# Modulation blocks of a four-layer transformer kernel at other places in TensorE's order

## The chip, the cores and the metric

The kernel runs on one core of a Trainium2 chip. The metric is the time of one execution on the device in microseconds (us); "before" is the median of three runs. The engines are TensorE (PE, matrix products), VectorE (DVE), ScalarE (ACT), GpSimd (POOL) and SyncE (SP, which here only issues transfers). Each has a queue of its own and works it off in order; a wait on a semaphore holds up everything behind it in that queue.

## What is computed

Two layers of a first block on 256 latent and 256 context tokens of width 1024, then two layers of a second block on the latent tokens alone. The change touches the first block:

```python
for i in range(DEPTH):                      # 2 layers
    mod_l = jnp.split((jax.nn.silu(c) @ w_mod[i] + b_mod[i])[:, None, :], N_MOD, axis=-1)      # 6 parts
    mod_c = jnp.split((jax.nn.silu(c_ctx) @ w_mod[i] + b_mod[i])[None, None, :], N_MOD, axis=-1)
    h_l = modulate(rms_norm(x, norm1_g[i]), mod_l[0], mod_l[1])
    h_c = modulate(rms_norm(ctx, norm1_g[i]), mod_c[0], mod_c[1])
    ...  # i == 0: diff_attention_mixer; i == 1: neighbourhood_mixer
    x = x + mod_l[2] * y_l
    x = x + mod_l[5] * squared_relu_mlp(modulate(rms_norm(x, norm2_g[i]), mod_l[3], mod_l[4]), w_mlp1[i], w_mlp2[i])
    ...  # the same for ctx with mod_c, in layer 0
```

`w_mod[i]` has 1024 x 6144 elements. The vectors `c` and `c_ctx` are the same for all tokens, so a product with it is two rows against a large matrix: the work lies in bringing its weights in: 24 blocks of 1024 x 256 elements a layer.

## The kernel before

All numbers are fp32. A product with full accuracy is made of three passes (`passes`, L802 where it issues the matmuls) over a weight block split into a high and a low part: ACT rounds a block of the ring to `Wh` (L1523), DVE writes the rest to `Wl` (L2044), each in two halves; the same is done to activations (`HTh`, `HTl`).

**The ring.** All weights of the program form one list, `blocks`, built by `first_weights` and `second_weights` in the order in which SP issues their transfers (L2806). The ring has RING = 3 slots of 1 MB; block i goes to slot i % 3, so its transfer waits until block i - 3 has left: when it is a split block, until DVE has split its second half (semaphore `w_split`), when it is a raw one, until PE has used it (`mod_used`). There are two buffers of split weights (SPLIT = 2).

**Modulation.** A modulation block is 256 columns of `w_mod`, a raw block of 1 MB. `modulation_block` (L956) multiplies it without a split, eight matmuls of 32 x 256 into the accumulator bank `mod_sum` (pa3), with `cT` on the other side. The first eight blocks of layer 0 are taken at the start, in another form. The 40 later ones (`LATER_MOD`) are called by `next_modulation(n)` from PE's program: n = 0 to 19 (`QK_MOD` = 20), one behind each tile of the first layer's query, key and value projections; n = 20 to 39 in steps of the first attention (`modulation_step`: steps 0, 1, 3, 5 and 6 of each eight). Blocks form groups (`MOD_GROUPS`); when one is complete, ACT copies its sums (`copy_group`), PE folds them (`fold_group`), ACT copies the result and DVE adds the bias (`add_group`) into `MOD`. DVE's `gains` makes the norms' factors from `MOD`. While groups are open, bank pa3 is theirs, and the pool A of accumulators has three banks in place of four (`A.width`); after the first attention it has four again.

**Norms.** In a norm PE sums the squares (`norm`, the matmuls with `con` and `Pb` or `Lb`), ACT makes the root, and DVE and ACT write eight normed tiles (`normed`, L2136, L1567, L2143). PE's first product behind a norm takes a tile as soon as it is there (`side_by_side`). Around a norm the order on DVE is: the first half of the second weight block (`prepare((0,))`, by `last=(0,)`), the root, the eight tiles, then the second half of that block (`prepare((1,))`).

**Near attention** (layer 1) has 16 steps of two heads each (`NEAR_STEPS`). Step s on PE is the scores of s, the transposes of s - 2 and the values of s - 3. Its bias tables come by `bias_rows(c)`, 16 transfers of 64 KB in pieces of 64 elements: c = 0 and 1 from POOL's queue, c = 2 and 3 from SP's, at the place in `blocks` that `late_bias` names, when the last value tile is complete.

## Time and profile before

| | us |
|---|---|
| median of three runs | 2641.91 (2641.17 to 2642.12) |
| profiled execution, its own time | 2639.67 |
| its span, first to last instruction | 2637.9 |
| PE busy | 2508.2 (95%) |
| DVE busy | 1701.9 (65%) |
| ACT busy | 1234.5 (47%) |
| POOL busy | 234.4 (9%) |
| TensorE's mean granted clock | 0.981 of 2.4 GHz |

In the trace the first layer's projections run from about 45 to 234 us, the first attention to 337, the second norm of layer 0 stands at 377, the first norm of layer 1 at 737, and the near attention runs from 879 to 937. A timeline row reads: start, duration, engine, line, operation, written <- read, and in brackets how long the engine was idle before it and what ended that. Matmuls overlap, so the time that one takes from PE is the distance between two starts, not its duration.

### The profile page before, as it was taken

How to read it: one execution, taken by the hardware profiler on the slowest of the kernel's cores; microseconds unless marked ns; L12 is line 12 of the kernel's file. 1: busy time of each engine (PE TensorE's matmuls, PEld its weight loads, DVE VectorE, ACT ScalarE, POOL GpSimd, SP SyncE). 2: the span in 40 equal slices, each digit the busy share in tenths (PEclk: the TensorE clock that was granted, in tenths of full speed). 3: DMA queues.
4: the chain of work that ended last, by engine and by line, in shares of the span. 5: the costliest groups of instructions: out<-in, count | busy, mean ns of one | idle time of the engine just before them, and what ended most of it. 6: DMA issues, size and time to landing. Idle time of an engine off the chain costs nothing.

```text
span 2637.9 us, 41664 instructions
## 1 busy us (share of the span) xinstructions
PE 2508.2 (95%) x16871; PEld 2221.6 (84%) x16871; DVE 1701.9 (65%) x3153; ACT 1234.5 (47%) x2228; POOL 234.4 (9%) x277
## 2 busy tenths in 40 slices
PE   6999989999989999999999999999999999999998
PEld 4666578888877689999989979899899899798997
DVE  4664855545575666677657677776676576777764
ACT  3433733223255554454444455554544444555443
POOL 1000010000053310000010012000000100120001
PEclk8999999999989999999999999999999999999999
DMA  7655723223235335556564525465765644254654
GB/s 269 208 172 193 225 77 112 96 96 96 96 89 119 80 111 164 164 173 176 166 173 148 153 74 176 128 192 162 206 177 168 172 147 154 77 175 128 189 166 122
DMA packets 497135, 393.74 MB, mean 149 GB/s; under 512 B 26168, under 2 KB 464704, under 8 KB 496048
## 3 DMA queue, kind: packets, MB, share of 16 engines
q1 hardware_dynamic: 494144, 384.92, 48.1%
q0 software_dynamic: 2080, 3.53, 1.1%
q8 instruction: 134, 2.20, 0.4%
q10 hardware_dynamic: 720, 2.62, 0.3%
q14 instruction: 57, 0.47, 0.1%
HBM read 389.99 MB, written 1.05 MB: 148 GB/s over the span
## 4 chain that ended last, share of the span: by engine, by line
PE 84%; DVE 9%; ACT 3%; issue 1%; SPq 1%; DMA 1%; POOL 1%; DVEq 0%; ACTq 0%
PE pv L802 35%; PE pa L802 31%; PE pv L1266 6%; PE pv L767 4%; PE pv L1265 3%; DVE Wl L2044 3%; PE pa L767 2%; PE pa L772 2%; ACT Wh L1523 1%; PE pa L956 1%; SPq L2790 1%; DMA BIG<-in_w_mod_dram 0%; DVE HTl L2051 0%; POOL BIG L2764 0%; DVE TMP L2136 0%
## 5 line engine op out<-in xcount | busy, mean ns | idle before, releaser
L2044 DVE TENSOR_TENSOR Wl<-ring,Wh 128x1024 fp32r<-128x1024 f32 (+4 forms) x688 | 757.8, 1142 | 269.6 <-ACT Wh L1523 266.2
L1523 ACT ACTIVATE Wh<-ring 128x1024 fp32r<-128x1024 f32 (+4 forms) x688 | 641.1, 980 | 497.1 <-PE pv L802 329.9
L802 PE MATMUL pa<-HTl,Wh 128*128 128x256 f32 (+1 forms) x1648 | 540.7, 328 | 34.8 <-DVE HTl L2143 20.9
L802 PE MATMUL pv<-HTl,Wh 128*128 128x256 f32 (+1 forms) x1872 | 539.3, 288 | 16.0 <-DVE T L2478 5.9
L802 PE MATMUL pv<-HTh,Wh 128*128 128x256 f32 (+1 forms) x1872 | 537.6, 287 | 0.0
L802 PE MATMUL pv<-HTh,Wl 128*128 128x256 f32 (+1 forms) x1872 | 537.5, 287 | 0.0
L802 PE MATMUL pa<-HTh,Wl 128*128 128x256 f32 (+1 forms) x1648 | 522.6, 317 | 0.0
L802 PE MATMUL pa<-HTh,Wh 128*128 128x256 f32 (+1 forms) x1648 | 522.0, 317 | 0.0
L802 PEld LDWEIGHTS pa<-HTl,Wh 128*128 128x128 f32 x1648 | 320.9, 195 | 69.0 <-issue 42.4
L802 PEld LDWEIGHTS pv<-HTl,Wh 128*128 128x128 f32 x1872 | 359.8, 192 | 21.8 <-issue 11.8
L802 PEld LDWEIGHTS pv<-HTh,Wh 128*128 128x128 f32 x1872 | 359.9, 192 | 2.5
L802 PEld LDWEIGHTS pv<-HTh,Wl 128*128 128x128 f32 x1872 | 359.9, 192 | 2.4
L802 PEld LDWEIGHTS pa<-HTh,Wl 128*128 128x128 f32 x1648 | 321.1, 195 | 20.3 <-issue 1.4
L802 PEld LDWEIGHTS pa<-HTh,Wh 128*128 128x128 f32 x1648 | 320.6, 195 | 18.5
L1266 PE MATMUL pv<-HID,Wh 128*128 128x512 f32 x704 | 246.9, 398 | 0.0
L2703 POOL TENSOR_TENSOR Pb<-Pb 128x256 f32<-128x256 f32 (+1 forms) x60 | 62.6, 1044 | 1452.9 <-ACT Pb L1534 1452.0
L1265 PE MATMUL pv<-HID,Wl 128*128 128x256 f32 x672 | 189.0, 281 | 0.0
L802 PE MATMUL pv<-HID1h,Wl 128*128 128x512 f32 (+1 forms) x512 | 172.1, 336 | 0.0
L802 PE MATMUL pv<-HID1l,Wh 128*128 128x512 f32 (+1 forms) x512 | 172.1, 336 | 0.0
L802 PE MATMUL pv<-HID1h,Wh 128*128 128x512 f32 (+1 forms) x512 | 172.1, 336 | 0.0
L2173 DVE SCALAR_TENSOR_TENSOR XT<-pv,MOD,XT 128x256 f32<-128x256 f32 x216 | 95.6, 479 | 112.0 <-PE pv L802 111.2
L1266 PEld LDWEIGHTS pv<-HID,Wh 128*128 128x128 f32 x704 | 130.6, 188 | 29.9
(277 smaller groups left out, 3309.5 us busy)
## 6 DMA issues: line engine op xcount, KB each, us to landing
ring<-in_ffn_w_gu_dram SPq DMA_DIRECT2D x176, 512.0 KB, 5.1
ring<-in_w_mlp_dram SPq DMA_DIRECT2D x64, 1024.0 KB, 5.3
ring<-in_ffn_w_down_dram SPq DMA_DIRECT2D x64, 704.0 KB, 4.6
ring<-in_w_in_dram SPq DMA_DIRECT2D x42, 1024.0 KB, 5.2
ring<-in_w_mod_dram SPq DMA_DIRECT2D x40, 1024.0 KB, 5.6
ring<-in_a_w_qkv_dram SPq DMA_DIRECT2D x12, 1024.0 KB, 5.2
ring<-in_b_w_qkv_dram SPq DMA_DIRECT2D x12, 1024.0 KB, 5.2
ring<-in_w_out_dram SPq DMA_DIRECT2D x8, 1024.0 KB, 5.1
```

The lines of the kernel that those rows point to most:

```text
L767: m = nc.tensor.matmul(o, lhsT=lhsT, rhs=rhs, start=start, stop=stop)
L772: m = nc.tensor.transpose(o, x, C("ident"))
L802: m = nc.tensor.matmul(o, lhsT=x, rhs=y, start=first and j == 0, stop=last and j == 2)
L956: m = nc.tensor.matmul(mod_sum[32 * j:32 * j + 32, 0:256], lhsT=cT[:, k, 30 - 2 * at:62 - 2 * at], rhs=w[:, k, :], start=at == 0 and k < 4 ...
L1265: nc.tensor.matmul(b[:, 0:S], lhsT=wl[:, k, :], rhs=HID2h[:, kk, :], start=False, stop=False)
L1266: m = nc.tensor.matmul(b.rearrange("p (a n) -> p a n", a=2), lhsT=wh[:, k, :], rhs=HID2[:, :, kk, :], start=kk == 0, stop=kk == 2 * half - 1)
L1523: ins = nc.scalar.activation(Wh[rows, p % SPLIT, a:b], ring[rows, i % RING, a:b], ACT.Copy)
L2044: ins = v.tensor_tensor(Wl[rows, p % SPLIT, a:b], ring[rows, i % RING, a:b], Wh[rows, p % SPLIT, a:b].bitcast(F32), ALU.subtract)
L2173: m = v.scalar_tensor_tensor(XT[:, k, half], b[:, at:at + S], MOD[:, i, gate * KT + k, w:w + 1], XT[:, k, half], ALU.mult, ALU.add)
L2703: nc.gpsimd.tensor_tensor(a, a, squares(k)[:, 0:N], ALU.add).then_inc(sum_ready, 1)
L2790: sp.dma_start(dst, I["w_mod"][0][k * P:(k + 1) * P, a * width:(a + 1) * width]).then_inc(mod_in[k], 16)
```

## The change

The 40 later modulation blocks are placed anew: 8 with the projections (at the places `QK_PLACES`), 16 in the first attention (every second step, without step 16), 3 behind the sums of the second norm of layer 0, 3 behind those of the first norm of layer 1, 10 in steps 1 to 10 of the near attention. In the list of transfers the three of a norm stand behind the two weight blocks of the product that follows it; those of the near attention stand behind the first two of its output weight's four blocks. The groups of blocks and the steps at which they are copied, folded and added follow. With it:

- Pool A keeps three banks until step 15 of the near attention; one of the four value tiles of layer 1 goes to pool V and is copied by DVE.
- SP issues the bias tables ahead of the near attention's modulation blocks: c = 2 before the first three, c = 3 before the other seven. It waits for the value tile in pool V.
- `cT`, `modtwo`, `modt` and `fold` lie in the place of the last constants, which are loaded in the MLP of layer 1 (`last_consts`, `const_last`); "ones" is half as wide.
- Layer 1's gains of the second norm are made behind the near attention.

```diff
-QK_MOD = 20
+QK_PLACES = (0, 1, 3, 6, 9, 12, 15, 17)
+QK_MOD = len(QK_PLACES)
+HOLE_MOD = 3
...
-    places = (0, 1, 3, 5, 6)
-    n = QK_MOD + i // 8 * 5 + (places.index(i % 8) if i % 8 in places else -99)
-    return n if QK_MOD <= n < LATER_MOD else None
-
-
-MOD_GROUPS = ((0, FIRST_MOD), (FIRST_MOD, 16), (FIRST_MOD + 16, 16), (FIRST_MOD + 32, 8))
...
+    n = i // 2 if i < 16 else 8 + (i - 18) // 2
+    return QK_MOD + n if i % 2 == 0 and i != 16 and n < 16 else None
+
+
+AFTER_DIFF = QK_MOD + 16
+NEAR_MOD = AFTER_DIFF + 2 * HOLE_MOD
+MOD_GROUPS = ((0, FIRST_MOD), (FIRST_MOD, 16), (FIRST_MOD + 16, 8), (FIRST_MOD + 24, 16))
...
+                modulation_columns(QK_MOD, AFTER_DIFF)
+                by_columns(I["a_w_o"][0], 0, D)
             else:
-                by_columns(w, 0, 2 * D)
+                by_columns(w, 0, 512)
+                modulation_columns(NEAR_MOD - HOLE_MOD, NEAR_MOD)
+                by_columns(w, 512, 2 * D)
                 for c in range(2):
                     halves_of_rows(w, 2 * D + c * 512, 512)
-            by_columns(I["a_w_o" if i == 0 else "b_w_o"][0], 0, D)
-            if i == 1:
-                late_bias.append(len(blocks))
+                by_columns(I["b_w_o"][0], 0, 512)
+                late_bias.append(len(blocks) - 1)
+                modulation_columns(NEAR_MOD, NEAR_MOD + 3)
+                late_bias.append(len(blocks) - 1)
+                modulation_columns(NEAR_MOD + 3, LATER_MOD)
+                by_columns(I["b_w_o"][0], 512, D)
+                last_consts.append(len(blocks) + 6)
             n = CHUNK * P
             for c in range(FF1 // n + 1):
                 if c < FF1 // n:
                     by_columns(I["w_mlp1"][i], c * n, (c + 1) * n)
+                if c == 0 and i == 0:
+                    modulation_columns(AFTER_DIFF, AFTER_DIFF + HOLE_MOD)
...
-            return [(V if i == 0 and t == 3 else A, ("v", i, c, t)) for t in range(4)]
+            return [(V if t == 3 else A, ("v", i, c, t)) for t in range(4)]
...
+                    if 1 <= s <= LATER_MOD - NEAR_MOD:
+                        next_modulation(NEAR_MOD + s - 1)
...
+                    if s == NEAR_FOLDED:
+                        fold_group(3)
+                        A.width = BANKS
...
                     norm(("n1", i), ALL)
+                    for n in range(NEAR_MOD - HOLE_MOD, NEAR_MOD):
+                        next_modulation(n)
...
                 if i == 0:
-                    pe.wait_ge(mod_copied, len(MOD_GROUPS))
-                    A.width = BANKS
+                    A.width = BANKS - 1
                 norm(("n2", i), tc)
+                if i == 0:
+                    for n in range(AFTER_DIFF, AFTER_DIFF + HOLE_MOD):
+                        next_modulation(n)
...
-                    sp.wait_ge(a_full, A.nth(("v", 1, 1, 3)))
-                    for c in (2, 3):
-                        for dst, src in bias_rows(c):
-                            sp.dma_start(dst, src).then_inc(bias_late[c - 2], 16)
+                    c = late_bias.index(i)
+                    sp.wait_ge(v_full, V.nth(("v", 1, 1, 3)))
+                    for dst, src in bias_rows(2 + c):
+                        sp.dma_start(dst, src).then_inc(bias_late[c], 16)
+                if i in last_consts:
+                    sp.wait_ge(mod_added, len(MOD_GROUPS))
+                    sp.dma_start(con[:, LAST_CONST:CONST_W], I["pack"][:, LAST_CONST:CONST_W]).then_inc(const_last, 16)
```

SP's queue from the first attention's last modulation blocks to the MLP of layer 0, before; a row is a transfer into the ring, with its shape, what it waits for, and how many follow each other (`w_mod` modulation, `a_w_o` the output weight, `w_mlp` the MLP's two weights):

```order
L2806 DMA ring<-in_w_mod_dram 128x8x256 [waits mod_used] x19
L2806 DMA ring<-in_a_w_o_dram 128x8x256 [waits mod_used] x3
L2806 DMA ring<-in_a_w_o_dram 128x8x256 [waits w_split]
L2806 DMA ring<-in_w_mlp_dram 128x8x256 [waits w_split] x4
L2806 DMA ring<-in_w_mlp_dram 128x4x512 [waits w_split] x2
```

The same, in the changed kernel:

```order
L2849 DMA ring<-in_w_mod_dram 128x8x256 [waits mod_used] x13
L2849 DMA ring<-in_a_w_o_dram 128x8x256 [waits mod_used] x3
L2849 DMA ring<-in_a_w_o_dram 128x8x256 [waits w_split]
L2849 DMA ring<-in_w_mlp_dram 128x8x256 [waits w_split] x2
L2849 DMA ring<-in_w_mod_dram 128x8x256 [waits w_split] x3
L2849 DMA ring<-in_w_mlp_dram 128x8x256 [waits mod_used] x2
L2849 DMA ring<-in_w_mlp_dram 128x4x512 [waits mod_used]
```

Three modulation blocks now stand behind the MLP's first two, each waiting for a split block to leave its slot; on PE they stand between the norm's sums (`pa<-Lb,con`) and the first product, and in layer 1 it is the same:

```order
L793 MATMUL pa<-Pb,con 128x512
L793 MATMUL pa<-Lb,con 128x512
L982 MATMUL pa<-ring,con 32x256 x24
L828 MATMUL pa<-HTl,Wh 128x512
L828 MATMUL pa<-HTh,Wl 128x512
```

That is PE in the changed kernel at the second norm of layer 0; the row of 24 is new there.

SP's queue around the near attention, before (`b_w_o` is its output weight, `b_rpb` the bias tables):

```order
L2806 DMA ring<-in_b_w_o_dram 128x8x256 [waits w_split] x4
L2806 DMA ring<-in_w_mlp_dram 128x8x256 [waits w_split]
L2813 DMA HTf<-in_b_rpb_dram 64x4x64 [waits a_full]
L2813 DMA HTf<-in_b_rpb_dram 64x4x64 x15
L2813 DMA Oa<-in_b_rpb_dram 64x4x64 x16
L2806 DMA ring<-in_w_mlp_dram 128x8x256 [waits w_split] x3
```

And in the changed kernel:

```order
L2849 DMA ring<-in_b_w_o_dram 128x8x256 [waits w_split] x2
L2856 DMA HTf<-in_b_rpb_dram 64x4x64 [waits v_full]
L2856 DMA HTf<-in_b_rpb_dram 64x4x64 x15
L2849 DMA ring<-in_w_mod_dram 128x8x256 [waits w_split] x3
L2856 DMA Oa<-in_b_rpb_dram 64x4x64 [waits v_full]
L2856 DMA Oa<-in_b_rpb_dram 64x4x64 x15
L2849 DMA ring<-in_w_mod_dram 128x8x256 [waits mod_used] x7
L2849 DMA ring<-in_b_w_o_dram 128x8x256 [waits mod_used] x2
```

The modulation blocks stand behind the bias transfers there, and half of the output weight behind them.

## Rows read from the trace of the kernel before

**Rows 1.** The page: the span, and TensorE's (PE's) busy time

```profile
span 2637.9 us, 41664 instructions
...
PE 2508.2 (95%) x16871; PEld 2221.6 (84%) x16871; DVE 1701.9 (65%) x3153; ACT 1234.5 (47%) x2228; POOL 234.4 (9%) x277
```

**Rows 2.** PE timeline, first projections, and values' end: start us, us, work [idle before]

```profile
96.76 1.07 PE L956 MATMUL pa<-ring,BIG 128*32 128x256 f32 x16
...
97.76 0.50 PE L802 MATMUL pa<-HTl,Wh 128*128 128x512 f32 x1
...
104.20 0.59 PE L767 MATMUL pv<-BIG,con 128*128 128x256 f32 x2
...
233.64 1.07 PE L956 MATMUL pa<-ring,BIG 128*32 128x256 f32 x16
```

**Rows 3.** Timelines of ACT and DVE, the first projections

```profile
96.55 2.00 ACT L1523 ACTIVATE Wh<-ring 128x1024 fp32r<-128x1024 f32 x2
...
102.51 0.75 DVE L2345 SCALAR_TENSOR_TENSOR BIG<-BIG,gq,RQ 128x512 f32<-128x512 f32 x1
```

**Rows 4.** Timelines of PE, SyncE's queue (SPq) and ACT, first attention

```profile
296.07 0.63 PE L772 MATMUL pa<-con,Pb 128*128 128x128 f32 x4 [0.77 <-DVE HTl L2215]
...
312.92 0.37 SPq L2806 DMA_DIRECT2D ring<-in_a_w_o_dram  x1
...
320.52 1.05 ACT L1523 ACTIVATE Wh<-ring 128x1024 fp32r<-128x1024 f32 x1
...
324.74 1.16 PE L767 MATMUL pa<-BIG,PT 128*128 128x128 f32 x8 [1.25 <-ACT PT L1600]
```

**Rows 5.** Timelines of PE, DVE and SPq, second norm of layer 0

```profile
383.65 0.77 PE L802 MATMUL pa<-HTl,Wh 128*128 128x512 f32 x1 [6.48 <-DVE HTl L2143]
...
388.91 0.51 PE L802 MATMUL pa<-HTl,Wh 128*128 128x512 f32 x1
...
394.93 1.22 DVE L2044 TENSOR_TENSOR Wl<-ring,Wh 128x1024 fp32r<-128x1024 f32 x1
...
396.18 0.37 SPq L2806 DMA_DIRECT2D ring<-in_w_mlp_dram  x1
...
397.20 0.39 PE L802 MATMUL pa<-HTl,Wh 128*128 128x512 f32 x1
```

**Rows 6.** Timelines of PE, DVE and SPq, first norm of layer 1

```profile
743.30 0.55 PE L802 MATMUL pa<-HTl,Wh 128*128 128x256 f32 x1 [5.90 <-DVE HTl L2143]
...
750.45 1.22 DVE L2044 TENSOR_TENSOR Wl<-ring,Wh 128x1024 fp32r<-128x1024 f32 x1
...
751.70 0.37 SPq L2806 DMA_DIRECT2D ring<-in_b_w_qkv_dram  x1
...
751.84 0.70 PE L767 MATMUL pa<-SQ,con 128*128 128x256 f32 x2 [0.39 <-ACT SQ L1721]
```

**Rows 7.** Timelines of ACT, SPq and PE, near attention

```profile
877.90 0.60 ACT L1600 ACTIVATE BIG<-pa 128x512 f32<-128x512 f32 x1 [2.12 <-PE pa L802]
...
882.28 10.60 SPq L2813 DMA_DIRECT2D HTf<-in_b_rpb_dram  x16
...
882.76 2.55 PE L767 MATMUL pv<-BIG 64*128 64x512 f32 x4 [2.02 <-DVE nm L2284]
...
892.92 11.34 SPq L2813 DMA_DIRECT2D Oa<-in_b_rpb_dram  x16
...
895.51 1.13 PE L767 MATMUL pv<-BIG 64*128 64x512 f32 x4
...
898.62 1.13 PE L767 MATMUL pv<-BIG 64*128 64x512 f32 x4
...
909.59 1.21 PE L772 MATMUL pa<-con,Pb 128*128 128x128 f32 x8 [0.35 <-DVE Pb L2291]
```

**Rows 8.** DMA issues: KB each, median us to landing; and a window's DMA share, GB/s

```profile
ring<-in_w_mod_dram SPq DMA_DIRECT2D x40, 1024.0 KB, 5.6
...
892.00:896.00 4.00, 4.00 (x40) 2.54 (x38) 3.23 (x13) 2.92 (x7) 1.30 (x2) 1.00 0.64 96
```

More of the change, by code:

```diff
@@ L126, in constant_pack @@
     put("eps", np.full((P, 1), EPS))
-    put("minus", -np.ones((P, P)))
+    t = np.arange(S)
+    qc, kc = p % GRID_W, t % GRID_W
+    start = np.clip(qc - NA_COLS // 2, 0, GRID_W - NA_COLS)
+    inside = (kc[None, :] >= start[:, None]) & (kc[None, :] < start[:, None] + NA_COLS)
+    back = p // GRID_W * GRID_W + GRID_W - 1 - qc
+    put("ncol", np.where(inside, 0.0, NEG)[back])
+    half = HEAD // 2
+    freq = np.power(np.float32(10000.0), -np.arange(half, dtype=np.float32) * np.float32(2.0 / HEAD)).astype(np.float32)
+    put("freq", freq[p % half][:, None])
     pb = np.zeros((P, P))
```

77 lines of the change are left out of this document (42 added, 35 removed).

## The prediction

> **What bounds the kernel now.** I read the page first, then TensorE's own timeline stage by stage, then the waits. TensorE (PE) is busy for 95% of the span [rows 1], so a stage is worth looking at only where PE stops, or where something PE does can leave its queue. A modulation block is 16 overlapping matmul records; in the projections of the first layer one runs from 96.76 to 97.76, so it holds PE for 1.00 us [rows 2]. The 40 later blocks are about 40 us of PE. All 40 stay; what changes is where they stand, and what must have happened before each of them. A block is not split: PE reads it straight from the ring, so it needs a landed transfer of 1 MB, issue to landing 5.6 us in the median [rows 8], and the transfer needs a free one of three ring slots.
>
> **Part 1, projections of the first layer: 20 blocks become 8.** PE runs there without a gap: block, eight steps of a tile, the sum of squares, the turned pairs, block [rows 2]. Twelve removals are worth 12 x 1.00 = 12.0 us, less two things. The last removed block, at 233.64, stands where PE would wait for the last value tile's copy on VectorE anyway [rows 2]; I count 0.2 of its 1.0 us. And behind the odd tiles the turned pairs become the next wait: there ScalarE first splits a weight block (96.55) and VectorE ends the tile's gain at 103.26, while PE comes at 104.20 [rows 2, 3]. That is 0.94 us of slack, and the block taken away is 1.00 us, so four odd tiles lose 0.1 to 0.2 us each, 0.6 in all. Sum: 12.0 - 0.8 - 0.6 = **-10.6 us**, from -12 (neither counts) to -8 (1 us lost at each of the four).
>
> **Part 2, first attention: 20 blocks become 16.** PE is the bound here too: its only waits in the steady part are of 0.77 us, once in eight steps [rows 4]. Before, the blocks of steps 0 and 1 cost nothing (PE would wait for the first softmax); afterwards those of step 0 and step 32 don't, the latter because PE waits 1.25 us near it [rows 4]. So 18 paid blocks become 14: -4.0. Against it: the output weight's first block takes the ring slot of the block of step 28, before that of step 27. It was issued at 312.92 and ScalarE split it at 320.52 [rows 4]; a step of 2.5 to 3.8 us later, plus 5.6 us, it lands at 321 to 322, and ScalarE stands before it for about 1.5 us with the transposed copies behind. Sum **-2.5 us**, from -4.5 to +1.
>
> **Part 3, the hole of the second norm of layer 0: three blocks.** PE stops at 377.17 and starts the next product at 383.65, 6.48 us later, when VectorE has written the first normed tile; three blocks of 1.00 us would fit [rows 5]. But the order of the transfers decides. The ring holds three blocks; in it stand o3, u0, u1 (the last block of the output weight, the first two of the MLP); behind them come the three modulation blocks. The first takes o3's slot, the second u0's, the third u1's. A slot of a split block is free when both halves are split, and VectorE does the second half of u1 only behind all eight normed tiles: 394.93 plus 1.22. The row of SyncE shows it: the block that now takes u1's slot is issued at 396.18 [rows 5]. In the new order that block is the third modulation block, and PE has it ahead of the first MLP product. It lands at 396.18 + 5.3 to 5.6 = 401.6; PE, at the low clock after 22 us of standing (the profile shows 12 matmuls at 0.43 us from 383.65 to 388.91, then 0.227 us), needs 1.6 us for the block and 12.5 us for the 48 matmuls of u0: 415.6. Now the next product follows at 397.20 [rows 5]. VectorE does not wait for PE in the norm, so nothing moves that transfer forward. **+18.5 us**, from +15 to +22 (landing 4.6 to 7 us, 1 to 3 us of clock).
>
> **Part 4, the hole of the first norm of layer 1: three blocks.** The same construction: the third block takes the slot of the second projection block, whose second half VectorE splits at 750.45 to 751.67, behind the normed tiles; SyncE issues at 751.70 [rows 6]. Two gain operations of about 0.2 us leave VectorE ahead of the norm, so 751.3; landed at 756.8; block and 48 matmuls, 5 us of it at the low clock, end at 765.1. Now the two tiles are through at 751.4 (743.30 plus 48 matmuls) [rows 6]. +13.7. In this layer the pool of accumulators also has three banks where it had four, since the modulation sum keeps the fourth: a product then waits for the root of the tile three before it. Behind odd tiles ScalarE needs copy, square, split and root (0.2 + 0.5 + 2.0 + 1.6 us) in a PE step of 3.3 us, some 0.9 us too much, once in the part where PE isn't held by VectorE already. **+14.7 us**, from +12 to +19.
>
> **Part 5, the near attention: ten blocks.** A step is 3.11 us of PE without a gap (895.51, 898.62) [rows 7], so a block in it costs its 1.00 us. Worse is the first. SyncE's queue is in order: the last value product ends at 877.9; now SyncE issues 16 bias transfers in 10.60 us and 16 more in 11.34 us [rows 7], and nobody waits for SyncE behind them. In the new order three modulation blocks stand behind the first 16 and seven behind the second 16, and PE has one in each of steps 1 to 10. So: bias issued 878.0 to 888.7, first block landed at 894.3, where PE has been waiting since 884.5; with the blocks at 897 and 901 (they share the transfer engines with the second bias set) the scores of step 4 start at 904.4 instead of 892.40. The second 16 are issued by 901.2, the fourth block lands at 906.7: 1.2 us more of wait. Seven blocks at 1.00 us: +7.0. Gone are PE's three short waits behind that, the first of them 0.35 us [rows 7], some 1.2 us. 12.0 + 1.2 + 7.0 - 1.2 = **+19.0 us**, from +12 to +26. The value tile that moves to VectorE delays the first scores from 878.76 to 882.4, under the same wait.
>
> The Trainium skill (DMA: Bandwidth & Descriptors, section on issuing engines not being separate DMA queues) says that the sequencer's time to initiate a DMA is usually small relative to the DMA itself. By that rule the first block would be on its way soon after 878 and this part would come to +7. The trace doesn't bear it out for bias pieces: 0.66 us each.
>
> **The rest** I count at nothing: the constants' order (the last ones are loaded in the MLP of layer 1, 300 us ahead of their use; the new 0.4 us issue stands among transfers that PE has two blocks ahead), the gains now behind the near attention (VectorE idles there until the first output product), three banks in the MLP of layer 0 (a product of 5.4 us there against a 0.6 us copy).
>
> **Sum.** -10.6 - 2.5 + 18.5 + 14.7 + 19.0 = **+39.1 us**. The profiled execution took 2639.67 us (span 2637.9 and 1.8 around it); 2678.8. The median of the three timed runs is 2.24 us above the profiled one, so I expect 2641.9 + 39.1 = **2681.0 us**.
>
> **Rivals.**
> A. *The blocks are there in time and the holes get filled* (faster). Speaks for it: the hole is 6.48 us long, two of the three blocks do find their slots free early, and while PE works it keeps its clock (the twelve slow matmuls, 2.4 us, would go in each hole). Against it: SyncE's issue at 396.18 and 751.70. It decides at whether the third block is landed by 383.65. Then part 3 is 0 to -2.4, part 4 +1 to -1.4, and if the blocks of the near attention come in time as well, that part is ten blocks less PE's two waits at its start (2.02 and 0.7 us [rows 7]), +7.3: -10.6 - 2.5 - 1.2 - 0.2 + 7.3 = -7 us, 2635. Chance 0.04.
> B. *The near attention hides its first block's wait* (the blocks go out before the bias, or the issues are quick): +7, total +27, 2669. Against it stands the queue's order. Chance 0.15.
> C. *The transfers get in each other's way*: bias rows are 256-byte pieces and kept the transfer engines 0.64 busy for 96 GB/s [rows 8]; with blocks between them each of the first four may land 3 us later, and the three banks cost a wait at every odd tile. +10 and +5, total +54, 2696. Chance 0.10.
> D. *Only one of the two holes stalls*, since something I read as a wait isn't one there: 2662 to 2666. Chance 0.05.
> The Trainium skill (TensorE: Matmul & The Clock Gate, section on HAM oscillation) advises to keep DMA waits out from between matmuls, since the engine runs at the low clock behind each. What the low clock takes is in the terms from the rows; the page alone would only add that PE comes out slow after every such wait.
>
> **How the numbers follow.** Forecast 0.66 (2671 to 2691), A 0.04, B 0.15, C 0.10, D 0.05. Range for 8 in 10: 2664 to 2695, which takes in B and most of C. A measurement of this kernel tells about 0.2% (5 us) from no change. Faster 0.03 (most of A), same 0.02 (the rest of it, and a near attention that eats its gain), slower 0.95.
>
> **What would show it.** In the new profile: PE idle for about 22 us before the third block of the first hole and 17 us in the second, released by the transfer into the ring, and SyncE's issue of that block right behind VectorE's split of the block two before; PE idle about 10 us after the second scores of the near attention, with 16 bias issues ahead on SyncE; the projections at 6.96 us a tile where no block stands. I am wrong if PE works through either hole, if the third block is issued before VectorE's normed tiles, or if the projections keep 7.96 us a tile.

## The result: 2.4% slower, 63 us where 39 were forecast

| | before | after |
|---|---|---|
| median of the timed runs, us (lowest to highest) | 2642.01 (2641.17 to 2645.80) | 2705.24 (2701.61 to 2707.09) |
| profiled execution, us (span) | 2639.67 (2637.9) | 2706.05 (2704.3) |
| mean granted clock of TensorE in it | 0.981 | 0.969 |

The ratio is 1.0241, with a 95% interval of 1.0229 to 1.0253. The direction and the two holes were right; the time lies 10 us above the range of the forecast. The page of the changed kernel, to be held against [rows 1]: PE has as many matmuls, is busy 8.5 us longer, and its share of the span falls from 95% to 93%. So nearly all of the loss is standing.

```profile
span 2704.3 us, 41666 instructions
...
PE 2516.7 (93%) x16871; PEld 2229.1 (82%) x16871; DVE 1705.5 (63%) x3155; ACT 1233.7 (46%) x2226; POOL 237.9 (9%) x277
...
PEclk8999989999989799999999999999999999999999
```

**Where the time went.** In both kernels ScalarE writes 688 halves of weight blocks (the tile Wh), in the same order. The start of the k-th one in a trace, less its start in the trace of before, is the distance that the kernel has lost up to there. Two such pairs, the first and last lines of the part behind the near attention (timeline of ACT; first before, then after):

```profile
943.87 2.01 ACT L1523 ACTIVATE Wh<-ring 128x1024 fp32r<-128x1024 f32 x2 [6.74 <-PE pv L802]
...
2349.03 2.01 ACT L1523 ACTIVATE Wh<-ring 128x1024 fp32r<-128x1024 f32 x2 [1.99 <-PE pv L802]
```

```profile
1000.50 2.01 ACT L1558 ACTIVATE Wh<-ring 128x1024 fp32r<-128x1024 f32 x2 [6.86 <-PE pv L828]
...
2415.47 2.01 ACT L1558 ACTIVATE Wh<-ring 128x1024 fp32r<-128x1024 f32 x2 [3.30 <-PE pv L828]
```

1000.50 - 943.87 = 56.6 and 2415.47 - 2349.03 = 66.4 us: 9.8 us are lost in stages that the prediction counted at nothing. The same difference at five marks (before's clock: 209, 342, 739, 878, 944, 2349 us) gives this table; every experiment below is read by it. Each column is what the stage added to the distance, in us, in one profiled execution.

| kernel | projections (to 209) | first attention | hole of norm 2, layer 0 | hole of norm 1 and projections, layer 1 | near attention | behind it | sum |
|---|---|---|---|---|---|---|---|
| forecast | -10.6 | -2.5 | +18.5 | +14.7 | +19.0 | 0 | +39.1 |
| after | -9.8 | +0.2 | +18.7 | +12.2 | +35.3 | +9.8 | +66.4 |
| e1_split_ahead | -11.1 | +0.7 | -0.2 | +3.6 | +33.5 | +8.4 | +34.9 |
| e2_bias_behind | -12.0 | -0.4 | +18.0 | +11.5 | +27.0 | +7.6 | +51.7 |
| e3_both | -13.0 | -1.6 | -1.2 | +2.9 | +26.5 | +8.3 | +21.8 |
| e4_delay | -2.3 | 0.0 | +0.1 | +0.1 | 0.0 | +41.0 (the added copies) | +38.8 |
| e5_even | -10.0 | -1.5 | +18.1 | +11.5 | +35.2 | +4.9 | +58.2 |
| e6_bias_pool | -10.1 | -0.4 | +18.0 | +11.5 | +27.4 | +7.3 | +53.6 |
| e7_all | -9.9 | 0.0 | -0.1 | +1.0 | +29.9 | +8.0 | +28.8 |
| e8_att_cut | -10.9 | -1.5 | +18.0 | +14.7 | +35.4 | +9.7 | +65.4 |
| e9_old_columns | -11.2 | 0.0 | +17.7 | +11.4 | +33.1 | +1.1 | +52.1 |
| e10_interleave | -9.3 | -0.4 | -0.9 | +3.0 | +20.3 | +7.8 | +20.4 |
| e11_holes_only | -0.5 | +1.1 | +0.1 | +1.0 | 0.0 | +2.5 | +4.2 |
| e12_small_blocks | -11.0 | 0.0 | +0.5 | +1.5 | +5.5 | +8.3 | +4.9 |
| e13_gap15 | -9.6 | +0.1 | +18.9 | +12.3 | +35.4 | +2.6 | +59.8 |
| e14_paid_places | -4.5 | +2.9 | -0.2 | +1.1 | -0.1 | +0.7 | 0.0 |
| e15_before_column | +0.5 | +0.1 | +0.2 | +0.1 | +0.4 | +10.2 | +11.4 |

The first column shows how far such numbers can be trusted: twelve kernels have the projections of the changed kernel (all but e4, e11, e14 and e15), and they lie between -9.3 and -13.0; e4 has those of the kernel before, and stands at -2.3. A difference under 3 us in one cell is not read as an effect.

Two marks need care. The first, at 209, lies ahead of the last three of the 20 places of the projections. ScalarE's first softmax of the first attention (237.23 before, 226.13 after) is the better border: counted there, the changed kernel has won 11.1 us in the projections and lost 1.5 in the first attention. And the mark at 739 is the write of a second half, which e1, e3, e7, e10 and e12 move ahead of the norm. By PE's last sums of that norm (736.81 before) e1 has +1.8 in the first hole and +1.6 behind it, where the table says -0.2 and +3.6; in the other four the same 2 us pass from the one column to the other.

**The holes**, to be held against [rows 5, 6]. First hole, timelines of PE, DVE and SyncE's queue:

```profile
367.50 1.94 PE L982 MATMUL pa<-ring,con 128*32 128x256 f32 x32
...
391.82 1.93 PE L982 MATMUL pa<-ring,con 128*32 128x256 f32 x16 [22.39 <-DMA ring<-in_w_mod_dram]
```

```profile
385.33 1.22 DVE L2081 TENSOR_TENSOR Wl<-ring,Wh 128x1024 fp32r<-128x1024 f32 x1
...
386.58 0.37 SPq L2849 DMA_DIRECT2D ring<-in_w_mod_dram  x1
```

Two blocks (32 records) run at once, PE stands for 22.39 us, and the third block's transfer is issued 0.03 us after VectorE has split the second half of the block two before it. The second hole is the same picture: 17.98 us, and an issue at 761.03 behind a split that ends at 761.00.

**The near attention**, against [rows 7]. PE's timeline, then SyncE's queue:

```profile
904.06 3.78 PE L793 MATMUL pv<-BIG 64*128 64x512 f32 x8 [4.41 <-DVE BIG L2063]
...
919.18 1.94 PE L982 MATMUL pa<-ring,con 128*32 128x256 f32 x16 [11.34 <-DMA ring<-in_w_mod_dram]
...
926.92 1.07 PE L982 MATMUL pa<-ring,con 128*32 128x256 f32 x16 [0.79 <-DMA ring<-in_w_mod_dram]
...
940.60 1.93 PE L982 MATMUL pa<-ring,con 128*32 128x256 f32 x16 [9.50 <-DMA ring<-in_w_mod_dram]
```

```profile
899.68 10.60 SPq L2856 DMA_DIRECT2D HTf<-in_b_rpb_dram  x16
...
910.32 6.11 SPq L2849 DMA_DIRECT2D ring<-in_w_mod_dram  x3
...
916.48 15.36 SPq L2856 DMA_DIRECT2D Oa<-in_b_rpb_dram  x16
...
931.88 11.08 SPq L2849 DMA_DIRECT2D ring<-in_w_mod_dram  x4
```

The first set of bias transfers takes SyncE 10.60 us, as before. But the three blocks behind it take SyncE 6.11 us (the third issue alone 4.84), the second bias set 15.36 us where it took 11.34, and there is a second long wait of 9.50 us before the fourth block, for which the forecast had 1.2. Blocks after a wait last 1.93 us, not 1.07: PE has fallen to the low clock. Stretches of 4 us there (PE, PEld, DVE, ACT, POOL busy; granted clock; share of the transfer engines; GB/s):

```profile
916.00:920.00 4.00, 0.82 (x8) 0.40 (x12) 0.00 (x0) 0.00 (x0) 0.00 (x0) 0.50 1.10 365
...
940.00:944.00 4.00, 3.40 (x23) 2.13 (x24) 0.00 (x0) 0.38 (x1) 0.00 (x0) 0.50 1.08 342
944.00:948.00 4.00, 4.00 (x32) 2.40 (x34) 0.94 (x4) 0.81 (x2) 0.00 (x0) 0.66 0.90 304
```

In the last microseconds before the first block lands (PE has it at 919.18) the transfer engines are taken up wholly.

### The profile page after: what moved, and what is told of

It reads as the page before. It is cut to its first block, busy times and chain, and to the rows that moved or that the text cites. A ratio compares the mean times of both kernels' runs of the same rounds, so it can differ in the third digit from the quotient of the medians.

```text
span 2704.3 us, 41666 instructions
## 1 busy us (share of the span) xinstructions
PE 2516.7 (93%) x16871; PEld 2229.1 (82%) x16871; DVE 1705.5 (63%) x3155; ACT 1233.7 (46%) x2226; POOL 237.9 (9%) x277
## 4 chain that ended last, share of the span: by engine, by line
PE 81%; DVE 9%; ACT 3%; SPq 2%; issue 2%; DMA 2%; POOL 1%; DVEq 0%; ACTq 0%; POOLq 0%
PE pv L828 34%; PE pa L828 29%; PE pv L1301 6%; PE pv L793 4%; PE pv L1300 3%; DVE Wl L2081 2%; PE pa L793 2%; ACT Wh L1558 2%; PE pa L798 1%; PE pa L982 1%; SPq L2856 1%; SPq L2833 1%; DMA ring<-in_w_mod_dram 1%; DVE TMP L2173 1%; DVE HTl L2180 1%
## 5 line engine op out<-in xcount | busy, mean ns | idle before, releaser
L828 PEld LDWEIGHTS pa<-HTh,Wl 128*128 128x128 f32 x1648 | 321.2, 195 | 20.4 <-issue 1.4
```

The source lines that it names most:

```text
L828: m = nc.tensor.matmul(o, lhsT=x, rhs=y, start=first and j == 0, stop=last and j == 2)
```

## Experiments

All runs were made beside runs of the kernel before on the same chip (medians 2640.75 to 2641.48 us), in four series.

**e1_split_ahead: who holds the third block of a hole**

```
-  residual_gated(o ..., last=(0,)); norm_mod(n2); prepare((1,))
+  residual_gated(o ..., last=(0, 1)); norm_mod(n2)          # the same for n1 of layer 1, and on ScalarE
```

> The changed kernel, but in both holes ScalarE and VectorE split the second half of the MLP's (the projections') second block ahead of the norm, not behind its eight tiles. Theory 1 (the third modulation block waits for that ring slot, as parts 3 and 4 of the prediction say): SyncE issues the third block some 2 us after the norm's squares, it lands 5.5 us later, and PE stands for 0 to 4 us before it in place of 22.4 and 18.0. The two holes give back 15 to 18 and 10 to 14 us, 28 in all, near 2677 us. The norm itself comes about 1.2 us later. Rival (the transfer is slow or queued for another reason, or PE's clock is the cost): the waits before the third block stay above 12 us and the time stays within 8 us of 2705.

Measured: 2674.91 us, ratio 1.0127 [1.0112, 1.0142], 30 us below the changed kernel. PE's timeline at the two holes:

```profile
374.27 1.93 PE L982 MATMUL pa<-ring,con 128*32 128x256 f32 x16 [5.65 <-DMA ring<-in_w_mod_dram]
```

```profile
737.15 1.94 PE L982 MATMUL pa<-ring,con 128*32 128x256 f32 x16 [6.49 <-DMA ring<-in_w_mod_dram]
```

The waits fell from 22.39 and 17.98 to 5.65 and 6.49 us, a little longer than the 4 us of the expectation, and SyncE issued the block at 368.94. The two holes, the second with its projections, now cost 1.8 and 1.6 us in place of 18.7 and 12.2. So the cause of parts 3 and 4 is shown: the slot, freed by a split that stood behind the norm.

**e2_bias_behind and e3_both: the order on SyncE**

```
   by_columns(b_w_o, 0, 512)
-  [16 bias] M0 M1 M2 [16 bias] M3 ... M9
+  M0 M1 M2 [16 bias] M3 M4 M5 [16 bias] M6 ... M9          # M: a modulation block's transfer
```

> The changed kernel, but on SyncE the first three modulation blocks of the near attention stand ahead of the first 16 bias transfers, and the next three ahead of the second 16. Theory 1 (what the near attention pays is the order on SyncE, with 16 issues of 0.66 us or more in front of the blocks): the waits of 11.34 and 9.50 us are gone, that stage comes to 7 to 12 us above the kernel before in place of 34.9, and the time to some 2680 us. Rival (bias pieces and blocks get in each other's way in the transfer engines whatever the order): PE still stands for 5 us or more at a block of this stage, the stage stays above +20 and the time above 2690.

> Both edits at once. If the two causes are independent, the gains add: 28 + 25 us below the changed kernel, near 2652 us, and what is left over the kernel before is the late part (some 10 us) and the blocks that PE pays. If an earlier stage only hands its wait to the next, the gains don't add, and the time stays above 2665.

Measured: 2693.18 us (1.0200 [1.0183, 1.0218]) and 2665.15 us (1.0089 [1.0074, 1.0104]). The gains of the two edits add (30 + 12 against 40), though e3_both stays at the 2665 us that the expectation had named for the opposite: the second edit is worth 12 us and not 25. But the near attention only fell from 35.3 to 27.0 and 26.5, not to 7 to 12. In e3_both PE has the first three blocks at once, then waits 5.36 us for the fourth and 7.48 us for the seventh. The rival of e2_bias_behind had said just that: over 5 us at a block, stage above +20, time above 2690.

**e6_bias_pool: the bias transfers on GpSimd's queue**

```
-  sp.wait_ge(v_full, ...); 32 x sp.dma_start(bias)
+  pool.wait_ge(v_full, ...); 16 x pool.dma_start(bias)       # ahead of its steps; then 4 in each of steps 0 to 3
```

> The changed kernel, but GpSimd's queue issues the last 32 bias transfers, 16 ahead of its first step of the near attention and four in each of its first four steps; SyncE has only blocks. Theory 1 (the order on SyncE is what the near attention pays): PE's waits of 11.34 and 9.50 us before blocks are gone, what is left is 10 us of blocks, the 4.4 us wait for the value tile and 1 to 2 us of low clock, +12 us over the kernel before in that stage in place of +34.9: near 2682 us. Rival (the transfers get in each other's way in the engines): with the bias set in flight at the same moment PE still waits 5 us or more before a block, and the stage stays above +20.

Measured: 2697.26 us (1.0212 [1.0196, 1.0227]), the stage +27.4. No block is waited for any more; PE waits for GpSimd, which scales the second head's softmax. GpSimd's timeline, and the wait on PE:

```profile
897.60 9.18 POOL L2779 DMA_DIRECT2D HTf<-in_b_rpb_dram  x15 [35.06 <-PE pv L828]
914.94 0.62 POOL L2779 DMA_DIRECT2D HTf<-in_b_rpb_dram  x1 [8.15 <-issue]
...
918.02 0.70 POOL L2786 TENSOR_SCALAR Pb<-Pb,rr 128x512 f32<-128x512 f32 x1
```

```profile
918.78 1.12 PE L798 MATMUL pa<-con,Pb 128*128 128x128 f32 x4 [9.05 <-POOL Pb L2786]
```

Fifteen issues run in a row (0.61 us each), then the queue stands for 8.15 us before the sixteenth. I take it that something behind the issues is full; no row says what. Both theories missed: the waits left the blocks, as the first said, and the loss stayed, as the second said.

**e7_all: four edits at once** (the splits ahead, GpSimd's queue, the even column of e5, and on VectorE)

```
-  prepare(); copy_in(value_tiles(1, 1)[3])
+  copy_in(value_tiles(1, 1)[3]); prepare()
```

> Four edits at once: the splits ahead of the norms, the last bias transfers by GpSimd, the even column, and VectorE copies the last value tile ahead of its split of the output weight's block (in the changed kernel PE waits 4.41 us for that copy at the first scores). If all four causes are as I take them, they add: 2665 (both first edits) less 15 to 19 in the near attention less 5 to 7 late, 2638 to 2645 us, level with the kernel before. If it stays above 2650, one of the causes isn't what I take it for.

Measured: 2668.85 us (1.0107 [1.0092, 1.0122]), 24 us more than expected. Two of the four causes weren't what I took them for: the near attention stayed at +29.9 (PE waits 13.85 and 6.09 us for GpSimd's products behind its issues), and the even column did nothing. The copy did its part: the wait before the first scores went from 4.41 to 1.08 us.

**e10_interleave and e12_small_blocks: issue time or transfer time**

```
+  M0 M1 M2 [8 bias] M3 [4 bias] M4 [4 bias] ... M8 [4 bias] M9    # e10, with the edits of e1 and the copy of e7
+  block_of(..., (0, 1, ...))  for M0 to M9                        # e12: one row tile of eight is loaded
```

> The changed kernel with the splits ahead of the norms and the value tile's copy first, and with SyncE's queue of the near attention mixed: three blocks, eight bias transfers, block, four bias transfers, block, and so on. Theory 1 (a bias transfer costs its queue 0.6 to 0.7 us wherever it is issued, and what is paid is only what stands in a row ahead of a block or of GpSimd's own steps): four of them, 2.7 us, fit into a step of 4.1 us, PE's waits before blocks fall below 1 us, and the stage costs 8 to 12 us over the kernel before (26.5 with three blocks in a row ahead of 16 transfers); near 2649 us. Rival (transfer engines): waits of 5 us or more stay before blocks or products, the stage stays above +20, the time above 2660.

> The kernel e10 with one difference: each of the ten blocks' transfers in the near attention loads only the first of its eight row tiles (128 KB of 1 MB); the other seven tiles are left out, and PE multiplies what the slot held. Issues, waits and matmuls are the same in number. Theory 1 (blocks of 1 MB and bias pieces share the transfer engines, which are the bound of that stage: SyncE's first issue behind each block took 2.3 to 3.6 us in place of 0.62): these long issues vanish, PE's waits of 5.01 to 0.8 us before blocks go, the stage costs 10 to 12 us over the kernel before in place of 20.3; near 2650 us. Rival (the issues themselves on one queue are the bound): the waits stay, and the time stays within 3 us of 2660.

Measured: e10_interleave 2659.99 us (1.0070 [1.0058, 1.0083]), stage +20.3, not 8 to 12, with a wait of 5.01 us before a block, as the rival had said. SyncE's queue in it:

```profile
874.63 5.34 SPq L2860 DMA_DIRECT2D HTf<-in_b_rpb_dram  x8
880.01 0.60 SPq L2851 DMA_DIRECT2D ring<-in_w_mod_dram  x1
880.66 4.42 SPq L2860 DMA_DIRECT2D HTf<-in_b_rpb_dram  x4
885.12 0.60 SPq L2851 DMA_DIRECT2D ring<-in_w_mod_dram  x1
885.77 5.52 SPq L2860 DMA_DIRECT2D HTf<-in_b_rpb_dram  x4
```

The first eight bias issues take 0.67 us each. Once blocks are between them, four take 4.42 to 6.04 us, since one issue behind each block takes 1.7 to 3.6 us. The six blocks issued between bias transfers take 9.1 to 10.2 us from issue to landing (5.6 in the median of the kernel before [rows 8]), and PE's step of 4.1 us has become one of 5.0 to 6.4. Then e12_small_blocks, the same issues with an eighth of the blocks' bytes: 2643.57 us (1.0009 [1.0000, 1.0018]), stage +5.5 (less than the 10 to 12 of the expectation), no wait before any block, and 3.6 to 4.7 us from issue to landing. Its queue:

```profile
878.72 0.60 SPq L2854 DMA_DIRECT2D ring<-in_w_mod_dram  x1
879.37 2.59 SPq L2863 DMA_DIRECT2D HTf<-in_b_rpb_dram  x4
882.00 0.60 SPq L2854 DMA_DIRECT2D ring<-in_w_mod_dram  x1
882.64 2.58 SPq L2863 DMA_DIRECT2D HTf<-in_b_rpb_dram  x4
```

This decides it. With the bytes the six groups of four cost 4.4 to 6.0 us (5.2 in the mean), without them 2.6 to 3.1: what is paid is transfer time that blocks and bias pieces share. 32 bias transfers of 0.66 us and ten blocks of about 2.6 us (5.2 less 2.6, an estimate) are 21 + 26 = 47 us of transfers, for a stage of 16 steps whose blocks PE wants within the first eleven. The Trainium skill (DMA: Bandwidth & Descriptors, section on issuing engines not being separate DMA queues) says that transfers of all issuing engines end on the same 16 DMA engines. e6 agrees: with the bias on another queue the waits moved to another engine, and the stage only fell from 35.3 to 27.4 us. The +5.5 of e12 is ten blocks of 1.00 us, less 1.8 us of PE's waits in the stage (5.0 before, 3.1 in e12), less what the kernel before pays there at the low clock and e12 doesn't. That leaves 2.7 us for the clock; from the rows it is 0.49 x 3.33 + 0.36 x 4.00 = 3.1, an estimate:

```profile
884.00:888.00 4.00, 3.33 (x12) 1.69 (x10) 3.82 (x18) 3.17 (x9) 1.13 (x2) 0.51 0.98 288
888.00:892.00 4.00, 4.00 (x24) 2.33 (x26) 2.17 (x11) 2.44 (x7) 0.82 (x2) 0.64 0.70 120
```

```profile
880.00:885.00 5.00, 5.00 (x58) 3.05 (x51) 3.65 (x17) 3.44 (x9) 0.98 (x1) 1.00 0.65 122
```

The first two rows are the kernel before, the last is e12.

**e4_delay, e5_even, e9_old_columns, e13_gap15, e15_before_column: the 9.8 us behind the near attention**

```
e4   before: + for _ in range(100): step(v.tensor_copy(NT, XT[:, 0]))   # behind the near attention
e5   after:  + put("gap", zeros((P, 1)))    ahead of "halves", 1 column at the end
e9   after:  + put("gap", zeros((P, 255)))  ahead of "halves", 1 column at the end
e13  after:  + put("gap", zeros((P, 15)))   ahead of "halves", 1 column at the end
e15  before: "freq" (1 column) put ahead of "halves"
```

> The kernel before with one addition: 100 copies of 128x512 on VectorE, one behind the other, between the near attention and the next residual, about 60 us in which PE stands. No work of the stages behind it is changed. Theory 1 (the late 9.8 us of the changed kernel are PE's clock, which depends on when a short wait falls): the distance to the kernel before grows or falls by 2 to 10 us between that point and the end, in steps right behind waits of 2 to 3 us, at a lower granted clock. Rival (the late 9.8 us come from the change's own edits: constants, banks, gains): the distance stays the same within 1 us up to the end.

Measured: 2679.20 us (1.0144 [1.0129, 1.0160]). PE stood for 38.15 us more; the distance was 38.65 us at 994 and 38.65 to 38.8 at the end. This shift costs nothing later, so the first theory fell: the 9.8 us had to come from the change's own edits. That sent me to the durations, line by line, of the stages behind. One difference stands out. The page's groups of GpSimd's products with the constant "before" (a mask), in the kernel before and in the changed one:

```profile
L2769 POOL TENSOR_TENSOR TMP<-TMP,con 128x512 f32<-128x512 f32 x10 | 11.2, 1121 | 9.0 <-ACT TMP L1912 8.9
L2764 POOL TENSOR_TENSOR BIG<-BIG,con 128x512 f32<-128x512 f32 x10 | 10.9, 1092 | 388.8 <-DVE BIG L2569 388.8
```

```profile
L2812 POOL TENSOR_TENSOR TMP<-TMP,con 128x512 f32<-128x512 f32 x10 | 13.1, 1308 | 8.5 <-ACT TMP L1949 8.5
L2807 POOL TENSOR_TENSOR BIG<-BIG,con 128x512 f32<-128x512 f32 x10 | 12.7, 1267 | 389.2 <-DVE BIG L2612 389.2
```

The change packs the constants anew, and this mask went from column 1666 to 1667 of the tile `con`.

> The changed kernel with one empty column more ahead of the constant matrix of half turns, and one at the end of the pack: the mask that GpSimd multiplies with in the later mixers stands at an even column again (1668; it is at 1667 in the changed kernel and at 1666 in the kernel before). No instruction is added. Theory 1 (the late loss comes from that odd column: GpSimd's product takes 1.3 us in place of 1.1, PE's wait before the turned pairs grows from 1.79 to 2.08 us, and PE falls to its low clock behind it): these products take 1.1 us again, the steps at the third and at the last mixer stages go, the late part shrinks by 5 to 7 us, and the time comes to 2698 to 2700. Rival (the late loss has to do with the banks' order or with the moment in time): GpSimd's products or PE's waits stay as they are, and the time stays within 2 us of 2705.

> The changed kernel with 255 empty columns ahead of the constant matrix of half turns and one at the end: the mask of GpSimd's later products stands at column 1922, exactly 256 columns (1024 bytes a partition) behind its place in the kernel before, and every tile that is allocated behind the constants has its old address again. No instruction is added. With the mask at 1667 and at 1668 the products took 1.27 and 1.31 us in place of 1.09 and 1.12. Theory 1 (the addresses of the operands set the products' time, a single even column wasn't it): the products take 1.09 and 1.12 us again, PE's late waits are 1.79 and 1.54 us, the late part falls from 9.8 to 2 to 4 us, the time to 2698 to 2700. Rival (something else of the change slows GpSimd there, such as what runs beside it): 1.27 and 1.31 us stay, and the time stays at 2702 to 2706.

> The changed kernel with 15 empty columns ahead of the matrix of half turns and one at the end: the mask stands at column 1682, 16 columns (64 bytes) behind its place in the kernel before; the tiles behind the constants move by 16 columns too. Theory 1 (what counts is the place within 64 bytes: 1666, 1682 and 1922 are alike in that, 1667 and 1668 not): the products take 1.09 and 1.12 us, and the time is 2696 to 2700. Rival (a longer distance, up to 1024 bytes, or another tile's place counts): 1.27 and 1.31 us, 2702 or more.

> The kernel before with one column of the constants, the frequencies, moved ahead of the matrix of half turns: GpSimd's mask stands at column 1667 as in the changed kernel. Nothing else is moved. Theory 1 (this alone makes the late part): the products take 1.27 and 1.31 us, PE's late waits are 2.08 and 1.72 us, PE falls to the low clock behind them, the offset to the kernel before is 0 up to the first mixer and grows to 5 to 8 us by the end: 2646 to 2649. Rival (the late part needs something else of the change as well): less than 2 us.

Measured: e5_even (column 1668) 2701.85 us (1.0233 [1.0218, 1.0248]), products still 1.27 and 1.31 us: being odd isn't it. e9_old_columns (1922) 2695.97 us (1.0208 [1.0194, 1.0222]), products 1.09 and 1.12, the part behind the near attention +1.1 in place of +9.8. e13_gap15 (1682) 2697.46 us (1.0211 [1.0196, 1.0227]), products 1.09 and 1.12, that part +2.6. And e15_before_column, the kernel before with the mask at 1667: 2651.62 us (1.0039 [1.0026, 1.0051]), 10 us slower where 5 to 8 were expected, +10.2 in the same part. (Five other constants, from the half turns on, moved by one column with it.)

```profile
L2769 POOL TENSOR_TENSOR TMP<-TMP,con 128x512 f32<-128x512 f32 x10 | 13.1, 1308 | 10.2 <-ACT TMP L1912 10.2
L2764 POOL TENSOR_TENSOR BIG<-BIG,con 128x512 f32<-128x512 f32 x10 | 12.7, 1268 | 389.2 <-DVE BIG L2569 389.2
```

Not all of that part is the mask's. These products run from 1534 us on, and up to 1535 of before's clock e15 has already lost 3.0 us, the changed kernel 2.7, in steps that come back below. From 1535 to 2425 every one of the eleven traces with the mask at 1667 or 1668 loses 6.9 to 7.4 us (e5 7.4, e15 7.2, the changed kernel 7.1), and the five others lose -0.2 to +2.1 (e9 -0.2, e11 -0.1, e4 and e13 0.0, e14 +2.1). So the mask's place costs about 7 us, and the rest of the 9.8 is something else. That also settles e5, whose cell of +4.9 looks like half a cure: its products are slow, and it lacks the steps.

Twenty products of 0.18 us more are 3.6 us. What they do is seen on PE, which waits for them before its turned pairs. PE's timeline and a stretch of 4 us (PE, PEld, DVE, ACT, POOL busy; granted clock; DMA share; GB/s), first of the kernel before, then of e15:

```profile
1569.26 1.56 PE L767 MATMUL pv<-BIG,con 128*128 128x256 f32 x6 [1.54 <-POOL BIG L2764]
...
1568.00:1572.00 4.00, 2.74 (x18) 2.59 (x19) 2.40 (x7) 0.59 (x1) 2.14 (x2) 1.00 0.00 0
```

```profile
1574.26 2.81 PE L767 MATMUL pv<-BIG,con 128*128 128x256 f32 x6 [1.72 <-POOL BIG L2764]
...
1572.80:1576.80 4.00, 2.54 (x7) 2.07 (x7) 1.28 (x5) 0.61 (x1) 2.50 (x2) 0.70 0.00 0
```

Two waits, 1.78 and 1.54 us, are now 2.09 and 1.72 us. Behind the second PE falls from full speed to a granted clock of 0.70 (it was 1.00), and at the low clock the stretch lasts 1.8 us longer. The same trace has two such steps in each of the two later layers, 1.8 and 1.4 us, then 1.7 and 1.4. PE's waits for these products grow by only 2.3 us in sum (9.2 to 11.5); the larger part of the 7 us is the clock.

**e8_att_cut: is PE the bound of the first attention?**

```
-  for k in range(KT):
+  for k in range(1 if cut else KT):       # cut: 13 of the 16 blocks of the first attention
```

> The changed kernel without seven of the eight matmuls of 13 of its 16 modulation blocks in the first attention (their products are left out; the transfers and all waits stay). Theory 1 (PE is the bound there, as part 2 of the prediction says): 13 x 0.87 = 11.3 us less in that stage. Rival (VectorE and ScalarE set the pace of the steps, and a block taken away comes back as a wait, which is why four blocks fewer brought nothing): PE's waits in that stage grow by 8 us or more, and the stage is 0 to 3 us shorter.

Measured: the profiled execution took 2704.96 us and its stage -1.5 us, against +0.2 in the changed kernel; -0.4 and -1.5 also stand in the table for kernels with the blocks whole (e2, e5). PE's waits in the stage grew by some 2 us (from 9.8 to 11.7), and what is cut is less than I had counted: a block of 2 records still holds PE for 0.55 us (256.29 to 256.84), a whole one for 1.00. So 13 x 0.45 = 5.9 us were there to be had. The timed median, 2698.06 us (2695.94 to 2704.96; 1.0213 [1.0196, 1.0230]), is 7 us below the changed kernel's, which the profiled run is not. The two disagree. The profiled execution is the slowest of the four, and the granted clock in it is 0.94 over 288 to 316 us, behind waits of 1.2 us, where the changed kernel has 1.00 over 289 to 319; that alone hides some 1.7 us (an estimate, 0.06 of 28). So a part of the 5.9 us is real, and how much stays open. 11.3 us, the claim of part 2, it isn't.

**e11_holes_only and e14_paid_places: a spread from the findings**

```
+  HOLE_MOD = 2;  20 blocks in the first attention;  none in the near attention;  constants as in e9
+  QK_PLACES = 0 to 15                                            # e11
+  QK_PLACES = 0 to 19 without 4, 8, 12 and 14                    # e14
```

> A spread that follows from the findings: blocks with the projections at the first 16 of 20 places, 20 in the first attention as in the kernel before, two (not three) in each of the two holes, none in the near attention; the constants at the old addresses as in e9, the value tile's copy first. Theory 1: two blocks find their slots free and their transfers landed, so PE has them while it would stand: the holes cost 0 to -2 us each; the projections save 3 us, the three banks of layer 1 and the value tile cost 1 to 2 us; 2636 to 2642 us, level with or a little under the kernel before. Rival (each hole pays something even with two blocks, since the next weights come later): 2645 or more.

> The kernel e11 with other places in the projections: there the blocks at the last four places were taken out, and nothing was saved (PE stands at them anyway); here those at places 4, 8, 12 and 14 are. Theory 1 (a block in the steady part holds PE for 1.00 us): 3.5 to 4 us less than e11's 2642.6, thus 2638 to 2639.5, 0.05 to 0.15% under the kernel before. Rival (PE waits there for VectorE or ScalarE as soon as the block goes): 2641 or more.

Measured: e11_holes_only 2642.61 us (1.0006 [0.9997, 1.0015]), e14_paid_places 2639.39 us (0.9997 [0.9988, 1.0005]): neither can be told from the kernel before, though e14 has the lower median by 2 us. PE's timeline at the first hole of e11:

```profile
377.71 1.93 PE L981 MATMUL pa<-ring,con 128*32 128x256 f32 x32
...
384.26 0.77 PE L827 MATMUL pa<-HTl,Wh 128*128 128x512 f32 x1 [4.61 <-DVE HTl L2181]
```

Two blocks fill 1.9 us of the 6.48 us [rows 5] and cost nothing, +0.1 us in the first hole and 1.0 in the second with its projections. But they also don't bring PE back at the high clock: its first matmul behind the wait takes 0.77 us, as before. With the projections, what the blocks were worth is read between equal points. From the block at place 3 to the block at place 15 the kernel before takes 95.56 us, e11, with all of them, 95.56, and e14, with four fewer, 90.83: 1.2 us a block. From place 15 to the first softmax e14, with all four of the last places, takes 59.88 us and e11, with none, 57.02. So e11's four places were not free either, as its -0.5 in the table (taken ahead of three of them) seems to say and as the expectation of e14 took over. At the first softmax the two kernels stand at -3.0 and -4.5 us, and the first attention took 3.6 and 2.9 of it back. PE's waits between 222 and 345 us are 8.1 and 8.2 us in them, 5.5 in the kernel before, most of the growth before transposes that wait for VectorE. That e14 came out in its expected range is in part luck: more was won in front, and a loss that nobody had counted took it back.

## Why the prediction was wrong, point by point

**Part 1, projections, -10.6:** measured -9.8 at the mark of 209, -11.1 at the first softmax, right. From place 3 to place 15 eight blocks fewer brought 7.9 us, 0.98 each (95.56 to 87.70). That PE stands at the last place anyway is borne out too: without that block it waits 0.99 us for VectorE at 223.63.

**Part 2, first attention, -2.5:** measured +0.2, and +1.5 from the first softmax on. The step that failed is "PE is the bound here too". Before and after, the groups of transposes and their waits on PE in that stage (busy, mean ns, idle ahead of them):

```profile
L772 PE MATMUL pa<-con,Pb 128*128 128x128 f32 x96 | 17.3, 289 | 2.4 <-DVE HTl L2215 2.3
```

```profile
L798 PE MATMUL pa<-con,Pb 128*128 128x128 f32 x96 | 17.7, 295 | 5.5 <-DVE HTl L2252 4.1 <-ACT PT L1635 0.7 <-DVE Pb L2247 0.5
```

Four blocks went, 3.1 us of waits came: PE waits for VectorE to free the accumulator of the turned output. The other part is the clock at the start of the stage: the granted clock is 0.94 over 229 to 259 us, 1.00 over 238 to 268 before, some 1.8 us by an estimate (0.06 of 30). At ScalarE's ninth softmax instruction (245.66 before) the changed kernel has lost 2.0 us since the first, and e1, e2, e5 and e9, whose clock stays at 1.00, 0.5. A PE row without gaps had hidden that the next engine was less than a block behind.

**Part 3, first hole, +18.5:** measured +18.7, with the wait of 22 us and the issue behind the split as described; e1 shows the cause.

**Part 4, second hole, +14.7:** measured +12.2 up to the end of the projections; the hole itself cost 15.6 us (from 9.1 to 24.7), and 3.4 us were won back behind it, where PE had been waiting for VectorE's part. The one microsecond for three banks is inside this and can't be told apart.

**Part 5, near attention, +19.0:** measured +35.3; this step carries most of the miss. The mechanism named (blocks behind bias issues on SyncE) is real, and the first scores came where they were put (882.4 + 21.35 of distance = 903.8; 904.06). Mis-sized was the time of a transfer. "First block landed at 894.3" took 5.6 us from issue to landing; it was 8.9 (910.32 to 919.18). "The second 16 are issued by 901.2, the fourth block lands at 906.7" let three blocks of 1 MB and 16 bias transfers pass almost side by side; they had to share engines that were taken up wholly (1.10 in the row above), SyncE was through with the second 16 at 931.84 (910.5 in the forecast's clock, which had 901.2), and PE had the fourth at 940.60, that is 12.5 us later. Of the miss of 16.3 us that is 12.5. Of the 3.8 us left, the two rows at 940 and 944 account for some 3.1: PE is busy for 3.40 and 4.00 us in them at a clock of 0.50 and 0.66, that is 1.7 and 1.4 us lost (an estimate). Rival C, "the transfers get in each other's way", was the right one, with +10 for it where some 15 us were due: e12 takes 14.8 us off e10 by taking bytes away. I gave it 0.10, because I read issue time (0.66 us each) as a property of the queue; [rows 8] had shown the transfer engines at 0.64 with bias alone, with a block's share still to come.

**The rest, 0:** measured +9.8. "The constants' order" had been counted by its transfers alone. That the place of an operand in SBUF can change the time of a product was not thought of; e15, e9 and e13 show it, and it is about 7 us here. The rest of the 9.8 is 2.7 us of steps ahead of those products: two steps of 1 to 1.7 us stand at 1040 and 1069 us of before's clock in ten traces (after, e1, e3, e7, e8, e9, e11, e12, e13, e15), the second of them at least, but not in e2, e4, e5, e6, e10 and e14, behind waits of the same 2.92 and 2.55 us. What decides there whether PE keeps its clock is open. They are all of e13's 2.6 us in that column, and of e11's 2.5.

**The sum:** the forecast missed the profiled distance by 27.3 us: 16.3 in part 5, 9.8 in the rest, 3.5 in parts 1 and 2 together, -2.3 in parts 3 and 4. Between the medians the miss is 24.1 us (63.2 against 39.1).

## What to carry to other kernels

Before moving a transfer of 1 MB into a stage, add up the transfer engines' time of everything that must land there (here 0.66 us a bias transfer and about 2.6 us a block) and hold it against the stage's length; other orders and queues moved the waits and lowered the loss from 35.3 to 20.3 us at best, and only fewer bytes brought it to 5.5. A block put into a hole is free only if its ring slot is released ahead of the hole, so count the slots, not only the microseconds. And when constants are packed anew, compare the durations of the same instruction in both traces: a shift of one column made 20 products 17% longer, PE's waits for them grew by 2.3 us, and with PE's clock behind them the kernel lost 7.

## What the runs showed of the hardware

- GpSimd's fp32 product of 128x512 with a constant from SBUF takes 1.09 us with the constant at columns 1666, 1682 and 1922 of its tile, and 1.27 us at 1667 and 1668 (before, e13, e9; after, e5). PE's waits for the products grow with them, 1.78 to 2.09 us. The fast three are alike in their place within 16 columns (64 bytes). In e15 the mask of 256 columns that moved from 2690 to 2691 went from 0.63 to 0.73 us as well. Other places weren't tried.
- A wait of PE that grew from 1.54 to 1.72 us, 8 us behind one that grew from 1.78 to 2.09, was followed by a granted clock of 0.70 in place of 1.00 over 4 us (e15). The price was 1.8 us, for 0.5 us more of waiting.
- 64 KB in pieces of 256 bytes hold a queue for 0.62 to 0.66 us, on SyncE as on GpSimd. Behind a 1 MB block one issue takes 1.7 to 3.6 us; with 128 KB in its place mostly 0.62. GpSimd stood for 8.15 us before an issue behind fifteen in a row.
- A 1 MB block took 9.1 to 10.2 us from issue to landing with four bias transfers between blocks (e10), 5.6 in the median of the kernel before. The transfer engines moved 365 GB/s at a share of 1.10, and 96 GB/s at 0.64 with the 256-byte pieces alone.
